# Eighty unused values in front of the arena of a two-block transformer kernel with product-key experts

## What is computed

```python
def _peer(xn, w_q, subkeys, u_tab, v_tab):      # per layer; 256 tokens, 8 heads
    q = (t @ w_q).reshape(n_tok, 8, 2, 128)
    sc = einsum("thpd,hpnd->thpn", q, subkeys)   # two scores lists of 128 keys a head
    sv, si = top_k(sc, 16)
    cand = sv[:, :, 0, :, None] + sv[:, :, 1, None, :]
    top_v, pos = top_k(cand, 16)                 # 16 of 16384 experts a head and token
    idx = take_along_axis(cidx, pos); g = softmax(top_v)
    # for every token, its 8 * 16 experts, each a row u and a row v of 1024 values:
    h = einsum("cd,ced->ce", xc, take(u_tab, ic))
    a = gc * gelu(h)
    return einsum("ce,ced->cd", a, take(v_tab, ic))
```

## Time and profile before

| | us |
|---|---|
| median of the runs shown | 1840.67 |
| the profiled execution, its own time | 1841.62 |
| its span, first to last instruction | 1839.80 |
| TensorE busy | 1611.0 (88%) |
| VectorE busy | 1043.6 (57%) |
| ScalarE busy | 561.3 (31%) |
| GpSimd busy | 639.6 (35%) |
| mean DMA rate over the span | 349 GB/s |

### The profile page before, as it was taken

One profiled execution on the slowest core, in us unless ns is written; L12 is line 12 of the kernel. 1 busy time (PEld: TensorE's weight loads), 2 busy tenths in 40 slices (PEclk: granted clock), 3 DMA queues, 4 the chain that ended last, 5 costly groups with the idle time before them and its releaser, 6 DMA issues.

```text
span 1839.8 us, 19448 instructions
## 1 busy us (share of the span) xinstructions
PE 1611.0 (88%) x6410; PEld 955.7 (52%) x6410; DVE 1043.6 (57%) x2669; ACT 561.3 (31%) x1711; POOL 639.6 (35%) x538
## 2 busy tenths in 40 slices
PE   9999999999989888888888789898987888877776
PEld 7888886887444444443444236644443444322222
DVE  4111202128667766666766654875676677666664
ACT  2111000102334333333333333433343333333332
POOL 1000000004444454343554530243444454455543
PEclk9999999999999999999999999999999999999999
DMA  8334337528999999999999986899999999999996
GB/s 259 135 112 163 113 138 278 214 92 320 422 421 421 421 421 421 422 422 421 421 421 415 418 332 229 365 421 422 421 420 422 421 421 421 421 421 416 412 416 275
DMA packets 87263, 641.52 MB, mean 349 GB/s; under 512 B 9715, under 2 KB 11907, under 8 KB 16380
## 3 DMA queue, kind: packets, MB, share of 16 engines
q0 software_dynamic: 75840, 540.92, 71.4%
q1 hardware_dynamic: 11324, 99.38, 14.1%
HBM read 639.15 MB, written 1.11 MB: 348 GB/s over the span
## 4 chain that ended last, share of the span: by engine, by line
PE 44%; DMA 39%; DVE 7%; ACT 5%; issue 5%; POOL 1%; DVEq 0%; SPq 0%; POOLq 0%; ACTq 0%
DMA arena<-in_peer_uv,arena 38%; PE ps L1373 15%; PE ps L1000 8%; DVE arena L1906 4%; PE ps L1025 4%; PE ps L986 3%; PE ps L1234 2%; PE ps L1050 2%; PE ps L975 2%; ACT arena L844 1%; PE ps L1305 1%; PE ps L1208 1%; ACT arena L839 1%; PE ps L1295 1%; PE ps L1200 1%
## 5 line engine op out<-in xcount | busy, mean ns | idle before, releaser
L1373 PE MATMUL ps<-arena 128*128 128x512 f32 x2048 | 951.3, 609 | 206.7 <-ACT arena L844 206.5
L651 POOL DMA_INDIRECT arena<-in_peer_uv,arena x506 | 614.9, 1215 | 979.0 <-PE ps L1373 545.2
L1906 DVE CUSTOM_DVE_ANT_0 arena<-xn,arena 128x1024 f32<-128x1024 f32 x512 | 627.2, 1226 | 385.6 <-DMA arena<-in_peer_uv,arena 376.7
L1373 PEld LDWEIGHTS ps<-arena 128*128 128x128 f32 x2048 | 376.3, 192 | 719.2 <-issue 387.8
L834 ACT ACTIVATE arena<-arena 128x2 f32<-128x2 f32 x252 | 51.3, 204 | 780.8 <-DVE arena L1906 780.6
L844 ACT ACTIVATE arena<-const,arena 128x128 f32<-128x128 f32 x504 | 174.7, 394 | 8.2
L839 ACT ACTIVATE arena<-arena 128x1 f32<-128x1 f32 x504 | 121.3, 288 | 8.2
L1000 PE MATMUL ps<-hT,wbuf 128*128 128x256 f32 x512 | 111.5, 379 | 0.0
L1234 PEld LDWEIGHTS ps<-hT,wbuf 128*128 128x128 f32 x768 | 92.9, 192 | 21.9 <-issue 21.0
L1000 PEld LDWEIGHTS ps<-hT,wbuf 128*128 128x128 f32 x512 | 97.0, 190 | 13.3 <-DVE arena L1679 0.2
L1234 PE MATMUL ps<-hT,wbuf 128*128 128x128 f32 x768 | 93.4, 275 | 0.6 <-ACT hT L698 0.6
(11 more groups left out here) (242 smaller groups left out, 1222.4 us busy)
## 6 DMA issues: line engine op xcount, KB each, us to landing
wbuf<-in_blocks SPq DMA_DIRECT2D x26, 2048.0 KB, 8.9
wbuf<-in_heads SPq DMA_DIRECT2D x11, 1536.0 KB, 7.1
arena<-in_blocks SPq DMA_DIRECT2D x7, 2048.0 KB, 12.3
arena<-in_peer_uv,arena POOLq DMA_INDIRECT x518, 15.0
arena<-in_subk SPq DMA_DIRECT2D x2, 1024.0 KB, 8.1
arena<-bias_rows POOLq DMA_DIRECT2D x1, 2048.0 KB, 10.7
arena<-bias_rows SPq DMA_DIRECT2D x1, 2048.0 KB, 18.6
wbuf<-in_heads SPq DMA_DIRECT2D x3, 512.0 KB, 8.2
```

Source lines behind the costliest of these rows:

```text
L651: pool.indirect_dma_start(to, None, A[f"peer_uv{layer}"], bass.IndirectOffsetOnAxis(ap=expert[:, unit % 2, e:e + 1], axis=0))\
L1373: last = mm(ps[t][:, s * 512:(s + 1) * 512], diag[:, place(unit, e)], ring[:, place(unit, e), D + s * 512:D + (s + 1) * 512], start=(e == ...
L1906: last = nc.vector.tensor_tensor_reduce(out=ring[:, place(unit, e), 0:D], in0=xn[:, v // PEER_HEADS], in1=ring[:, place(unit, e), 0:D], sc ...
```

## The change

One buffer is allocated ahead of the arena. Nothing reads or writes it, and no view, wait, instruction or size is changed; every address in the arena becomes 320 bytes higher.

```diff
@@ -216,6 +216,7 @@
         root = sb("root", [P, TILES])
         rinv = sb("rinv", [P, TILES])
         small = sb("small", [P, 64])
+        sb("before_ring", [P, 80])
         arena = sb("arena", [P, 32128])
 
         ident = const[:, C_ID:C_ID + P]
```

## The result

The changed kernel takes 1822.11 us (median of four runs, 1821.19 to 1822.33) against 1840.76 us before on the same chip. The ratio is 0.9895, with a 95% interval of 0.9882 to 0.9907: 18.7 us, or 1.05%, faster. The forecast was 1840.7 us with a range of 1832 to 1845 and a chance of 0.14 for faster. The result lies outside the range, a little beyond the full form of the first rival (1824 us).

The account below looks back on a forecast made before the run. It took 1264 us of gather stages to be bound by DMA bytes, and TensorE to bound 0 to 420 us. All terms were zero, so 1840.7 us, the median before; range 1832 to 1845.

Parts of the forecast that it names:

- the first rival: Faster, placement of gather writes counts: partial form 1831 to 1837 us, full form 1824; chance 0.14 in all.
- The reading of the bound: Gather stages, 1264 us, go by bytes; each per cent in the gathers' service passes to the end as 12.6 us.
- The reads of TensorE: TensorE's reads of wbuf, late_w and the ring take the same time at offsets 128 and 192: zero.
- writes of the gathers: Ring moves from 192 to 0 past a multiple of 512; weight loads at 128, 192, 256 cost alike: zero.
- it may be hidden there: Argument for faster: late_w's 37.4 us a MB at 192 was measured with nothing beside it.
- The two lie at the same 192 bytes; the gap comes with what else differs: Gathers' 38.6 against late_w's 37.4 us a MB was put to shorter pieces and another queue, not placement.
- The upper end of the unknown: Reading the shares to their last half digit, w4 might be 0 to 0.8% cheaper than wbuf: up to 10 us gain.
- The page's rule: 256 byte transaction starts, if true for writes: 262 beats a row against 256, 2.3%, about 1812 us; outside the range.
- A slower gather at 512: Rival: row starts at multiples of 512 fall on the same spots more often; 1844 to 1865 us, chance 0.08.
- Places nothing: Rival: allocator lays the unused buffer elsewhere and the arena stays put; same time as forecast, counted inside "same", chance 0.78.

Follow-up runs that it names:

- light_ring_at_192: The kernel before with VectorE's row product cut from 1024 to 64 columns and TensorE's two products from 512 to 64 each: 1841.34 us.
- sp_rows: Kernel before and changed kernel, with gathers replaced by plain transfers of consecutive rows, issued by SP on queue 1: 1841.87 and 1822.74 us.
- direct_rows_at_192: The kernel before with indirect gathers replaced by plain transfers of 128 consecutive rows, same engine and queue: 1840.80 us.
- half_rows: Plain transfers of consecutive rows by GpSimd in 4096 byte pieces instead of 8192, in the kernel before and the changed kernel: 1877.61 and 1841.97 us.

## Why the prediction was wrong

**What held.** The reading of the bound: 1264 us that go by bytes, with enough gathers in line that a gain in their service passes to the end in full. A rise to 425 to 426 GB/s was priced at 16 us, and the stages did rise to these and the kernel gained 18.7. light_ring_at_192 confirms it from the other side, since taking most of the engines' work away changed nothing. The reads of TensorE were rightly put at zero; the first 420 us didn't move. w4, which lost its multiple of 256, cost nothing that can be seen, 78.3 us against 78.5, and 611.0 ns a piece.

**The step that failed** is the first of the change, "writes of the gathers": "Offsets of 128, 192 and 256 thus cost the same to half a per cent ... So I take zero." Three things were wrong in it.

- late_w at 192, alone on the engines, was the main witness against a price. It takes 37.4 us a MB at 192 and at 0. Its row was right, but it can't see the effect. The queue and the plain form, two of its differences to the gathers, are excluded by sp_rows; its longer pieces would halve the price and not hide it. Nor was there "nothing beside it": a load of wbuf ran until 305.2 us. What is left is that no gathers were there and that the stretch is short. The length may matter by itself, since the gathers too start nearly free of the price: in the kernel before 88% of their packets from 430 to 440 us take 309 ns, and 7% from 520 to 800 us (in the changed kernel 97% and 100%; in direct_rows_at_192 49% and 7%). That was not tried by itself. The prediction had it, "it may be hidden there", and gave it too little weight.
- w4 and wbuf, the only pair at 256 and 128 inside a full stage, did point the right way, 78.5 and 78.6 against 78.8 and 79.0. I took the 0.4% for the edge of what can be read, and even as an upper end carried it over to the gathers per cent for per cent. half_rows shows that the price goes by the piece: 0.4% at 16 KB is 0.8% at 8 KB, still short of 1.3%. The rest is that w4 was no free reference: it paid 1 to 1.5 ns itself among the gathers (612.5 ns against 611.0 after the change), and wbuf 3.7 (614.7 against 611.0, at its unchanged 128). The full 3.7 ns are 0.6% of a 16 KB piece, so 1.2% of one of 8 KB, near the 1.3% by which the rate rose.
- "The two lie at the same 192 bytes; the gap comes with what else differs" compared gathers with late_w, 38.6 against 37.4 us a MB. Of this gap of 1.2, 0.6 was the placement after all, since the gathers now take 38.0. The same offset doesn't give the same price in a stage that is full and in one that isn't.

The upper end of the unknown, 0.8% where 1.3% was measured, was therefore too low, and the range, which stopped at 1832, left out the case that came. Its full form stood among the rivals at 1824 with a chance of 0.04 or less.

**The page's rule.** The Trainium skill, in "DMA: Bandwidth & Descriptors", "How a descriptor splits into AXI transactions", has a transaction start at a multiple of 256 bytes; it says so of what is read. For the boundary the runs agree with it, for writes into SBUF too: 256 is as good as 0 (ratios 0.990 and 0.9895), 64, 128 and 192 are as bad as each other. I had written that the trace speaks against it for writes into SBUF; the writes were what moved here, and the gain came. As for the size, the rule would give 2, 4 and 6 beats more of 256 for 64, 128 and 192, so by an estimate from it 29 us at 192. Measured were 19 us, the same at all three, and more at 4 bytes past, where by the rule it is one beat. So the boundary of the page holds for these writes in a full stage, and its count of beats doesn't give their price, nor does it tell why a piece pays only beside others off the boundary.

**The other rivals.** A slower gather at 512 did not appear; the slow slices of before are rather fewer. "Places nothing" is excluded by the gain itself.

## What to carry to other kernels

Where a stage is kept full by transfers into SBUF, start each piece at a multiple of 256 bytes of the partition: it costs a few unused values, and was worth 1.05% here with 8 KB pieces and 1.9% with 4 KB pieces (1841.97 against 1877.61 us). To judge an offset from a trace, compare transfers inside equally full stages and count the price by the piece and not by the byte. A row of a short stretch without the stage's other transfers is no witness for the stage, even where the engines are as busy; and a load that shows a price may owe it to its neighbours.

## What the runs showed that was not expected

- Offsets of 64, 128 and 192 cost the same (ratios 0.9997, 0.9994 and 1), a start 4 bytes past a boundary more (1.0044).
- The price is not additive: with five places of nine off the boundary a quarter of it is left (0.9921 against 0.9895 and 1), and 87 to 93% of the packets take the aligned 309 ns.
- It takes two: the pieces of wbuf at an unchanged offset of 128 went from 614.7 to 611.0 ns when the gathers beside them were aligned, as short as with wbuf at 0.
- It is not there from the start: from 430 to 440 us 88% of the gathers' packets in the kernel before take 309 ns, from 520 to 800 us 7%.
- With TensorE at half its clock (0.50 from 1600 to 1700 us) and VectorE's products at 225 ns instead of 1226, the kernel took the same 1841 us.
- Open is what in the path of the writes makes the price. That loads without gathers show none, that mixed placements show little and that it comes up only some time into the stage are facts that an explanation would have to hold; none was tried here that does.
